# Second gate half and value compression in alternation, the linear attention's output gated and turned in two halves

## The chip, the cores and the metric

The kernel runs on one core of a Trainium2 chip. The metric is the device time of one execution in microseconds (us). The engines that matter are TensorE (PE: products and transposes), VectorE (DVE), ScalarE (ACT) and SyncE (SP), which here only issues loads. Each engine works through its own queue in order and waits on semaphores.

## The reference, cut to what matters

Two transformer layers on 256 tokens with a width of 2048, in float32. The first layer has four branches (pooling, spatial gating, window attention, convolution). The second has a sparse attention with compressed keys and values, a gated linear attention, a cross attention and a feed-forward part. This part of the second layer is what the change touches:

```python
def compress(u, pe, w1, w2):                 # u: 256 tokens, 2 heads; 15 blocks of 32 tokens
    blk = u[:, tok] + pe[None, None, :, None, :]
    blk = blk.transpose(0, 1, 3, 2, 4).reshape(B, n_cmp, HKV, -1)      # 4096 per block and head
    return (jax.nn.silu(blk @ w1) @ w2).transpose(0, 2, 1, 3)
kc = rms_norm(compress(k_cmp, pe_k, w_ck1, w_ck2), g_kc)
vc = compress(v_cmp, pe_v, w_cv1, w_cv2)
...
o_gla = gla_mixer(heads(q_l, GLA_HEADS) * (GLA_DK ** -0.5), heads(k_l, GLA_HEADS),
                  heads(v_l, GLA_HEADS), heads(log_a, GLA_HEADS))
o_gla = rms_norm(o_gla, g_gla_out).astype(x.dtype).reshape(B, T, -1) * jax.nn.silu(r_l)
x = x + jnp.concatenate([o_nsa, o_gla], axis=-1) @ w_out
```

Here `r_l` comes out of the layer's input projection, and is 1024 wide; the kernel makes it in two halves of 512 columns, `rl0` and `rl1`.

## The kernel before, in words

**Weights in chunks.** All large products are a list of `units` (one for each weight block, mostly 512 columns wide), and each unit is cut into `chunks` of 512 KB. One list, `chunks`, sets the order in which SP loads them, ScalarE and VectorE split them, and TensorE multiplies by them. A chunk lands in one of `NR` = 5 raw buffers (`raw`). ScalarE writes a rounded high part (`whi`, L404) and VectorE the rest (`wlo`, L405), into one of `NH` = 4 slots. TensorE then makes three products for each of two operand tiles and two halves of the tokens (L464): 12 for a chunk. The raw buffer is free once VectorE is done (`raw_free`), the slot once TensorE is. A chunk is split when TensorE's place in the list is at most four chunks before it.

**The compression's chunks.** `ck1` and `cv1` (keys and values, 8 chunks each) are used as they come, without a split: TensorE reads the raw buffer itself (`rows=32`, L422, eight instructions a chunk), so the raw buffer is freed by TensorE. Both read one operand buffer, `kp`. VectorE fills it for the keys, and again for the values (L1483) when ck1's last product is done. The result of cv1 is copied by ScalarE into `hid` (`use_hid`, L1150), and TensorE then folds it (`small_out`, L1492), the first step to the compressed values.

**PSUM banks.** Banks 0 to 3 belong to the units: a unit takes banks 2i and 2i + 1 with i the parity of its index, one for each half of the tokens. Its first product in a bank waits until the unit before it of the same parity has been read out (`slot_free`). Banks 4 to 7 are for the background work.

**Order around the change.** The units of the second layer's input projection are ql, ga, kl, vl0, vl1, q0, q1, ksvs, kcvc, kwvw, ck1, rl0, rl1, cv1. The eight chunks of ck1 alternate with the eight of rl0; then come the eight of rl1, and then the eight of cv1. The units wl0 to wl3 follow (`w_out` with the linear attention's half of its rows), then wp0 to wp3 (the sparse attention's half). wl0 has four chunks: its first two need operand tiles 0 to 3, the others tiles 4 to 7.

**Background threads.** Everything else is written as Python generators (`gla`, `compress`, `nsa_part` and others). `step()` advances each of them once, several times in a chunk, and so puts their instructions between the products; it does nothing while the planned clock of VectorE is over 3 us (`AHEAD`) ahead of TensorE's. The planner keeps a clock `now` for each engine, from estimated durations, and each signal has a due time (`when`). A thread holds an instruction back with `ready` until the due time of what it needs is 0.6 us past on TensorE's clock. If a chunk needs what is not yet written, `step(True)` advances all threads until it is. A load has no due time so far: it counts as landed.

**The end of the linear attention.** For each half `i`, once `rl{i}` and two heads' norms are there, `gla` multiplies the head outputs `vl` by the gate (L1443). When both halves are done it turns the result: `turn_seq` transposes two tiles at a time (L332) and splits them into the operand `oop` (ScalarE L314, VectorE L318). `oop` lies where the projection's operand lies, so a tile of it may only be written when rl1's product with the old tile is done (`hop_free`, set for the unit `LAST_IN2`, which is rl1).

**The names in the trace.** `t_raw`, `t_whi`, `t_wlo` are the weight buffers; `t_A` holds the operands; `t_H` here `vl` and `rl`; `t_Y0b` has `kp`; `t_R` has `hid`; `ps` is any PSUM bank.

Of the kernel before, what the change touches and what calls it, by code (L numbers as in the profile page):

```python
# [13 lines left out]
P = 128  # L14
# [38 lines left out]
for _i in range(4):  # L53
    for _n in range(4):
        S1[f"g{_i}{_n}"] = (10496 + _i * D + _n * 512, 10496 + _i * D + _n * 512 + 512)
S2 = dict(ql=(2584, 3096), kl=(3096, 3608), vl0=(3608, 4120), vl1=(4120, 4632), rl0=(4648, 5160), rl1=(5160, 5672),
          q0=(0, 512), q1=(512, 1024), kcvc=(1024, 1536), ksvs=(1536, 2048), kwvw=(2048, 2560))
# [9 lines left out]
def due(tok):  # L67

    if tok is None:
        return 0.0  # L70
    if isinstance(tok, list):
        return max([due(x) for x in tok] + [0.0])
    return tok[0].when.get(tok[1], 0.0)


def elements(pattern):
    n = 1
    for _, size in pattern.ap[1:]:
        n *= size
    return n  # L80
# [23 lines left out]
class Lane:  # L104
# [41 lines left out]
    def dma(self, out, in_, count, *tokens):  # L146
        self.wait(*tokens)
        count.value += 16
        self.engine.dma_start(out, in_).then_inc(count.sem, 16)
        return (count, count.value)  # L150


def build(nc, dr, out):
    ctx = ExitStack()
    with ctx:
        body(nc, dr, out, ctx)


def body(nc, dr, out, ctx):
# [39 lines left out]
    def at(reg, shape, dt=F32, off=0, name=None):  # L199
        names[0] += 1  # L200
        return nc.alloc_sbuf_tensor_at(name or f"t{names[0]}_{reg}", [P] + list(shape), dt, offset=where[reg] + int(off))
# [7 lines left out]
    def par(name, a=0, b=None):  # L209
        lo, hi = PP[name]  # L210
        return pp[:, lo + a:(hi if b is None else lo + b)]
# [14 lines left out]
    def ready(*toks):  # L226

        while max([due(x) for x in toks]) > T.now - 0.6:
            yield
# [12 lines left out]
    flags = {}  # L242
# [61 lines left out]
    def split_into(op, kt, n, src, tok, scale=1.0, scales=None, behind=None):  # L304

        if scales is None:
            a = S.do(lambda e: e.activation(op.hi[:, kt:kt + n, :], src, ACT.Copy, scale=scale), tok, behind)  # L307
            b = V.do(lambda e: e.scalar_tensor_tensor(out=op.lo[:, kt:kt + n, :], in0=src, scalar=scale,  # L308
                                                      in1=op.hi[:, kt:kt + n, :].bitcast(F32), op0=ALU.mult,
                                                      op1=ALU.subtract), a, behind)  # L310
        else:
            for k in range(n):
                sc = scales(kt + k)
                a = S.do(lambda e, k=k, sc=sc: e.activation(op.hi[:, kt + k, :], src[:, k, :], ACT.Copy, scale=sc),  # L314
                         tok, behind)
            for k in range(n):
                sc = scales(kt + k)
                b = V.do(lambda e, k=k, sc=sc: e.scalar_tensor_tensor(  # L318
                    out=op.lo[:, kt + k, :], in0=src[:, k, :], scalar=sc, in1=op.hi[:, kt + k, :].bitcast(F32),
                    op0=ALU.mult, op1=ALU.subtract), a, behind)  # L320
        for k in range(n):
            op.ready[kt + k] = b
        return b

    def turn_start(c, kt, src, tok):

        b = c.bank()
        ps = banks[b][:].rearrange("p (k n) -> p k n", k=2)
        T.wait(tok)
        for k in range(2):  # L330
            for t in range(NT):
                fn = lambda e, k=k, t=t: e.transpose(ps[:, k, t * P:(t + 1) * P], src(t, kt + k), ident)  # L332
                if k == 1 and t == 1:
                    got = T.do(fn)
                else:
                    T.silent(fn)
        return b, ps, got

    def turn_seq(c, op, kts, src, tok, scale=1.0, scales=None, behind=None, over=None):

        def finish():
            k0, b, ps, got = pend.pop()
            held = behind if over is None else [over[k0], over[k0 + 1]]
            c.tok = bg_free[b] = split_into(op, k0, 2, ps, got, scale, scales, held)

        pend = []
        for kt in kts:
            if len(c.pool) == 1 and pend:
                finish()
            while over is not None and kt + 1 not in over:  # L350
                yield
            yield from ready(tok, *[bg_free[b] for b in c.pool if len(c.pool) == 1])
            pend.insert(0, (kt,) + turn_start(c, kt, src, tok))
            if len(pend) > 1:
                finish()
            yield
        finish()


    units, chunks = [], []  # L360

    def unit(name, w, n, kts, op, use, rows=None, need=(), k0=0, flip=False):


        u = dict(name=name, w=w, n=n, kts=kts, op=op, use=use, rows=rows, index=len(units),
                 need=need, k0=k0, flip=flip)
        per = w.shape[2]
        assert kts % per == 0 and per * n <= 1024, (name, kts, per, n)
        for c in range(kts // per):
            chunks.append((u, c, per))  # L370
        units.append(u)
# [18 lines left out]
    hop_free = {}  # L390
# [728 lines left out]
    vl = at("H3", [NT, 1024])  # L1119
    rl = at("H4", [NT, 1024])  # L1120
    nq = at("M0", [NT, 1024])
    kcvc = at("M1", [NT, 512])
    ksvs = at("M1", [NT, 512], off=4096)
    kwvw = at("R0", [NT, 512])

    def rscale(t):
        return keepers[:, 2 + t:3 + t]

    def keep2(dst, name):
        def use(t, ps, tok):  # L1130
            d = dst(t)
            n = d.shape[-1]
            r = S.do(lambda e: e.activation(d, ps[:, 0:n], ACT.Copy, scale=rscale(t)), tok, last_use["rx"],
                     last_use["free2"])
            last_use[name] = r
            return r
        return use

    def in2(name, n, use):
        unit("2" + name, dr["w_in2"][name], n, 16, hop, use, need=("x1",))  # L1140
# [22 lines left out]
    def use_rl(i):  # L1163
        def use(t, ps, tok):
            d = rl[:, t, i * 512:(i + 1) * 512]
            a = S.do(lambda e: e.activation(d, ps[:], ACT.Tanh, scale=half_r[:, t:t + 1]), tok, last_use["rx"],
                     last_use["free2"])
            r = V.do(lambda e: e.scalar_tensor_tensor(out=d, in0=d, scalar=1.0, in1=ps[:], op0=ALU.add,
                                                      op1=ALU.mult), a)
            last_use[f"rl{i}"] = r  # L1170
            return r
        return use

    units2 = dict(
        ql=lambda: in2("ql", 512, keep2(lambda t: qlkl[:, t, 0:512], "ql")),
        kl=lambda: in2("kl", 512, keep2(lambda t: qlkl[:, t, 512:1024], "kl")),
        ga=lambda: unit("2ga", dr["w_in2"]["ga"], 40, 16, hop, use_ga, need=("x1",), flip=True),
        q0=lambda: in2("q0", 512, keep2(lambda t: nq[:, t, 0:512], "nq0")),
        q1=lambda: in2("q1", 512, keep2(lambda t: nq[:, t, 512:1024], "nq1")),
        vl0=lambda: in2("vl0", 512, keep2(lambda t: vl[:, t, 0:512], "vl0")),  # L1180
        vl1=lambda: in2("vl1", 512, keep2(lambda t: vl[:, t, 512:1024], "vl1")),
        kcvc=lambda: in2("kcvc", 512, keep2(lambda t: kcvc[:, t, :], "kcvc")),
        ksvs=lambda: in2("ksvs", 512, keep2(lambda t: ksvs[:, t, :], "ksvs")),
        kwvw=lambda: in2("kwvw", 512, keep2(lambda t: kwvw[:, t, :], "kwvw")),
        rl0=lambda: in2("rl0", 512, use_rl(0)),
        rl1=lambda: in2("rl1", 512, use_rl(1)),
        ck1=lambda: unit("ck1", dr["w_ck1"], 256, 32, lambda l: kp[:, l, :], use_hid("k"), rows=32),
        cv1=lambda: unit("cv1", dr["w_cv1"], 256, 32, lambda l: kp[:, l, :], use_hid("v"), rows=32, need=("hk",)))
    for name in "ql ga kl vl0 vl1 q0 q1 ksvs kcvc kwvw ck1 rl0 rl1 cv1".split():
        units2[name]()  # L1190


    at_ = next(i for i, x in enumerate(chunks) if x[0]["name"] == "ck1")
    chunks[at_:at_ + 16] = [chunks[at_ + 8 * j + i] for i in range(8) for j in range(2)]

    bT = at("Y1b", [4, 256])
# [13 lines left out]
    oop = Operand("A", 16)  # L1210
# [5 lines left out]
    def gla():  # L1216
        c = CG
# [111 lines left out]
        made, summed = {}, {}  # L1329
# [110 lines left out]
        for i in range(2):  # L1440
# [3 lines left out]
                out=vl[:, t, i * 512:(i + 1) * 512], in0=vl[:, t, i * 512:(i + 1) * 512], scalar=rscale(t),  # L1444
                in1=rl[:, t, i * 512:(i + 1) * 512], op0=ALU.mult, op1=ALU.mult) for t in range(NT)],
                after=last_use[f"rl{i}"])
            yield
        if "nsa4" in flags:
            c.pool = [4, 5]
        yield from turn_seq(c, oop, range(0, 8, 2), lambda t, k: vl[:, t, k * P:(k + 1) * P], c.tok,  # L1450
                            scales=lambda k: par("g_gla", k % 2, k % 2 + 1), over=hop_free)

        yield from norm(c, ckv[0][:].rearrange("p t (h d) -> p (t h) d", d=P), qlkl[:, 0, :].rearrange("p (h d) -> p h d", d=P))
        a = c.v(lambda e: e.tensor_scalar(par("g_cq"), par("g_cq"), P ** -0.5, None, ALU.mult))
# [392 lines left out]
    for d in range(len(chunks)):  # L1847
        u, c, per = chunks[d]
# [170 lines left out]
```

## Time and profile before

| | |
|---|---|
| runs | 2429.7, 2432.16, 2433.64 us, median 2432.16 |
| the profiled execution | 2432.07 us, its span 2430.7 us |
| TensorE busy | 2401.1 us (99%), granted clock 0.995 in the mean |
| VectorE, ScalarE busy | 1502.8 us (62%), 1118.3 us (46%) |
| loads | 186 GB/s in the mean |

The span is the time from the first to the last instruction of the execution that was profiled. A busy share of 99% says that what TensorE does in turn sets the time. Times below are us from the span's start. A line of a timeline has the start, the duration, engine, source line, operation, what is written and read, and the count; in brackets stands idle time before it with what ended it. Products overlap one another, so the starts give their pace, not the durations.

### The profile page before, as it was taken

Reading aid. Unit: us, or ns where it says so; the run is one execution under the profiler, and the core shown is the slowest. Engines: PE = TensorE matmul, PEld = TensorE weight load, DVE = VectorE, ACT = ScalarE, POOL = GpSimd, SP = SyncE. Lnnn points to the kernel's source line nnn. Section 1 sums busy time; section 2 is a strip of 40 time slices with the busy share of each in tenths; the row PEclk is TensorE's granted clock in tenths of the full one; section 3 lists DMA queues with packets and bytes.
Section 4 is the critical chain, followed back from the end, with each engine's and each line's share of the span. In section 5 each row is a group of like instructions: output and inputs, shape, how many; then the busy total and the mean of one; then the engine's idle time right before and its main releaser. Section 6 shows DMA issues by size and latency. Waiting matters only on the chain.

```text
span 2430.7 us, 28661 instructions
## 1 busy us (share of the span) xinstructions
PE 2401.1 (99%) x11302; PEld 1985.0 (82%) x11302; DVE 1502.8 (62%) x2122; ACT 1118.3 (46%) x1391; POOL 0.2 (0%) x4
## 2 busy tenths in 40 slices
PE   8999999999999999999999999998999999999999
PEld 7888888888888888888888887787888888888887
DVE  5566989865544554577667865776555555554443
ACT  5554444544444444454455654445444444444333
POOL 0000000000000000000000000000000000000000
PEclk9999999999999999999999999999999999999999
DMA  8545666666665766665544444553666666666664
GB/s 292 173 143 185 192 191 194 213 184 214 191 198 151 257 225 198 191 217 181 176 156 149 163 135 166 163 178 126 189 190 187 190 190 189 190 191 190 200 203 143
DMA packets 124227, 452.99 MB, mean 186 GB/s; under 512 B 13691, under 2 KB 15916, under 8 KB 123068
## 3 DMA queue, kind: packets, MB, share of 16 engines
q1 hardware_dynamic: 124092, 451.17, 60.0%
q8 instruction: 88, 1.44, 0.2%
q14 instruction: 47, 0.39, 0.0%
HBM read 448.99 MB, written 2.12 MB: 186 GB/s over the span
## 4 chain that ended last, share of the span: by engine, by line
PE 97%; DVE 1%; DMA 1%; ACT 1%; issue 0%; SPq 0%; DVEq 0%; ACTq 0%
PE ps L464 90%; PE ps L332 1%; PE ps L599 1%; PE ps L549 1%; PE ps L1408 1%; PE ps L582 0%; DVE t_wlo L405 0%; PE ps L513 0%; DMA t_raw<-w_out 0%; PE ps L989 0%; ACT t_whi L404 0%; PE ps L422 0%; PE ps L445 0%; DMA t_raw<-w_kv 0%; PE ps L1540 0%; PE ps L1578 0%
## 5 line engine op out<-in xcount | busy, mean ns | idle before, releaser
L464 PE MATMUL ps<-t_whi,t_A 128*128 128x512 f32 (+1 forms) x4992 | 1552.8, 393 | 10.2 <-DVE t_wlo L405 9.2
L405 DVE TENSOR_TENSOR t_wlo<-t_raw,t_whi 128x1024 fp32r<-128x1024 f32 x805 | 980.4, 1224 | 807.8 <-ACT t_whi L404 802.5
L404 ACT ACTIVATE t_whi<-t_raw 128x1024 fp32r<-128x1024 f32 x805 | 849.3, 1058 | 1043.5 <-PE ps L464 1026.4
L464 PEld LDWEIGHTS ps<-t_whi,t_A 128*128 128x128 f32 x4992 | 926.7, 189 | 200.9 <-DVE t_wlo L405 9.9
L464 PE MATMUL ps<-t_wlo,t_A 128*128 128x512 f32 (+1 forms) x2496 | 971.7, 389 | 0.0
L464 PEld LDWEIGHTS ps<-t_wlo,t_A 128*128 128x128 f32 x2496 | 470.6, 189 | 97.8
L464 PE MATMUL ps<-t_whi,t_Y0a 128*128 128x512 f32 x1152 | 355.9, 390 | 1.2 <-DVE t_wlo L405 1.2
L464 PEld LDWEIGHTS ps<-t_whi,t_Y0a 128*128 128x128 f32 x1152 | 215.3, 188 | 45.6 <-DVE t_wlo L405 1.7
L464 PE MATMUL ps<-t_wlo,t_Y0a 128*128 128x512 f32 x576 | 224.2, 389 | 0.0
L464 PEld LDWEIGHTS ps<-t_wlo,t_Y0a 128*128 128x128 f32 x576 | 108.1, 188 | 22.6
L883 DVE SCALAR_TENSOR_TENSOR t_Y1a<-t_H,t_pp,t_Y1a 128x255 f32<-128x255 f32 (+29 forms) x240 | 96.3, 465 | 0.0
L464 PE MATMUL ps<-t_whi,t_Y1a 128*128 128x512 f32 x256 | 79.3, 391 | 0.0
L464 PEld LDWEIGHTS ps<-t_whi,t_Y1a 128*128 128x128 f32 x256 | 47.6, 188 | 9.5
L464 PE MATMUL ps<-t_wlo,t_Y1a 128*128 128x512 f32 x128 | 49.8, 389 | 0.0
L332 PEld LDWEIGHTS ps<-t_cc,t_H 128*128 128x128 f32 x184 | 23.3, 145 | 10.6 <-DVE t_Y0a L308 2.5
L332 PE MATMUL ps<-t_cc,t_H 128*128 128x128 f32 x184 | 28.7, 281 | 2.3 <-DVE t_Y0a L308 1.6
L464 PEld LDWEIGHTS ps<-t_wlo,t_Y1a 128*128 128x128 f32 x128 | 24.0, 188 | 5.0
L308 DVE SCALAR_TENSOR_TENSOR t_Y0a<-ps,t_Y0a 128x512 fp32r<-128x512 f32 x30 | 20.5, 687 | 12.0 <-ACT t_Y0a L307 12.0
L307 ACT ACTIVATE t_Y0a<-ps 128x512 fp32r<-128x512 f32 x30 | 17.6, 589 | 19.5 <-PE ps L332 19.5
L698 ACT ACTIVATE t_W<-ps 128x512 f32<-128x512 f32 x32 | 19.1, 598 | 16.0 <-PE ps L464 16.0
L570 ACT ACTIVATE t_H<-t_H,t_st 128x128 f32<-128x128 f32 (+1 forms) x32 | 14.3, 447 | 23.7 <-DVE t_st L563 23.7
L314 ACT ACTIVATE t_A<-ps,t_pp 128x256 fp32r<-128x256 f32 x48 | 19.8, 470 | 9.9 <-PE ps L332 9.9
(290 smaller groups left out, 1097.5 us busy)
## 6 DMA issues: line engine op xcount, KB each, us to landing
t_raw<-w_in SPq DMA_DIRECT2D x376, 512.0 KB, 4.1
t_raw<-w_gu SPq DMA_DIRECT2D x176, 512.0 KB, 3.6
t_raw<-w_down SPq DMA_DIRECT2D x88, 512.0 KB, 4.2
t_raw<-w_branch SPq DMA_DIRECT2D x64, 512.0 KB, 4.1
t_raw<-w_out SPq DMA_DIRECT2D x64, 512.0 KB, 4.1
t_raw<-w_ck SPq DMA_DIRECT2D x16, 512.0 KB, 4.2
t_raw<-w_cv SPq DMA_DIRECT2D x16, 512.0 KB, 4.6
t_raw<-w_cq SPq DMA_DIRECT2D x8, 512.0 KB, 3.9
```

Of the source, the lines that this page charges most:

```text
L307: a = S.do(lambda e: e.activation(op.hi[:, kt:kt + n, :], src, ACT.Copy, scale=scale), tok, behind)
L308: b = V.do(lambda e: e.scalar_tensor_tensor(out=op.lo[:, kt:kt + n, :], in0=src, scalar=scale, in1=op.hi[:, kt:kt + n, :].bitcast(F32), op ...
L314: a = S.do(lambda e, k=k, sc=sc: e.activation(op.hi[:, kt + k, :], src[:, k, :], ACT.Copy, scale=sc), tok, behind)
L332: fn = lambda e, k=k, t=t: e.transpose(ps[:, k, t * P:(t + 1) * P], src(t, kt + k), ident)
L404: a = S.do(lambda e: e.activation(whi[:, s, 0:n], raw[:, d % NR, 0:n], ACT.Copy), tok, free)
L405: b = V.do(lambda e: e.tensor_tensor(wlo[:, s, 0:n], raw[:, d % NR, 0:n], whi[:, s, 0:n].bitcast(F32), ALU.subtract), a, free)
L464: fn = lambda e, x=x, w=w, kt=kt, k=k, t=t, j=j, bk=bk: e.matmul(bk[:, 0:n], x[:, u["k0"] + kt, t * P:(t + 1) * P], w[:, k, :], start=(kt ...
L549: c.pe([lambda e, h=h: e.matmul(banks[b][:, h * nk:(h + 1) * nk], scores(h)[0], scores(h)[1], start=True, stop=True) for h in range(nh)])
L599: c.pe([lambda e, h=h, k=k: e.matmul(banks[b][:, h * w:(h + 1) * w], PT[:, (h * nkt + k) * P:(h * nkt + k + 1) * P], values(h, k), start=( ...
L698: last_use[f"G{t}"] = S.do(lambda e: e.activation(G[:, t, :], ps[:], ACT.Tanh, scale=0.5), tok, last_use.get(f"G{t}"))
L883: fns.append(lambda e, x=x, y=y, w=w: e.scalar_tensor_tensor(out=y, in0=x, scalar=w, in1=y, op0=ALU.mult, op1=ALU.add))
L1408: summed[h, j] = c.pe([lambda e, i=i, w=w: e.matmul(ps3[:, :, i:16], con("sel", 16 - i, 144 - i), w, start=(i == 0), stop=(i == 15), skip_ ...
```

## The change

There are three edits. The units come in the order ck1, rl0, cv1, rl1, and the chunks of cv1 alternate with those of rl1, as those of ck1 do with rl0. In `gla` the turn moves into the loop over halves: half 0 is gated and its four tiles are turned and split, then half 1. In the planner, a load gets a due time: SP's clock, which advances by the load's size at 320 GB/s, plus 2 us. No instruction is added or taken away.

```diff
     def dma(self, out, in_, count, *tokens):
         self.wait(*tokens)
         count.value += 16
-        self.engine.dma_start(out, in_).then_inc(count.sem, 16)
+        made = self.engine.dma_start(out, in_)
+        self.now = max(self.now, due(list(tokens))) + elements(made.ins.outs[0]) * made.ins.outs[0].ap[0][1] / 80000
+        count.when[count.value] = self.now + 2.0
+        made.then_inc(count.sem, 16)
         return (count, count.value)
...
-    for name in "ql ga kl vl0 vl1 q0 q1 ksvs kcvc kwvw ck1 rl0 rl1 cv1".split():
+    for name in "ql ga kl vl0 vl1 q0 q1 ksvs kcvc kwvw ck1 rl0 cv1 rl1".split():
         units2[name]()


     at_ = next(i for i, x in enumerate(chunks) if x[0]["name"] == "ck1")
+    chunks[at_:at_ + 16] = [chunks[at_ + 8 * j + i] for i in range(8) for j in range(2)]
+
+    at_ = next(i for i, x in enumerate(chunks) if x[0]["name"] == "cv1")
     chunks[at_:at_ + 16] = [chunks[at_ + 8 * j + i] for i in range(8) for j in range(2)]
...
                 in1=rl[:, t, i * 512:(i + 1) * 512], op0=ALU.mult, op1=ALU.mult) for t in range(NT)],
                 after=last_use[f"rl{i}"])
             yield
-        if "nsa4" in flags:
-            c.pool = [4, 5]
-        yield from turn_seq(c, oop, range(0, 8, 2), lambda t, k: vl[:, t, k * P:(k + 1) * P], c.tok,
-                            scales=lambda k: par("g_gla", k % 2, k % 2 + 1), over=hop_free)
+            if "nsa4" in flags:
+                c.pool = [4, 5]
+            yield from turn_seq(c, oop, (4 * i, 4 * i + 2), lambda t, k: vl[:, t, k * P:(k + 1) * P], c.tok,
+                                scales=lambda k: par("g_gla", k % 2, k % 2 + 1), over=hop_free)
```

## Rows read from the trace of the kernel before

**Rows 1.** The page: the span, and each engine's busy time.

```profile
span 2430.7 us, 28661 instructions
...
PE 2401.1 (99%) x11302; PEld 1985.0 (82%) x11302; DVE 1502.8 (62%) x2122; ACT 1118.3 (46%) x1391; POOL 0.2 (0%) x4
```

**Rows 2.** TensorE's waits in all: engine, line, releaser; total us, times, longest.

```profile
PE ps L1492 <- ACT t_R L1150: 4.2, 1, 4.2
...
PE ps L422 <- DMA t_raw<-w_cv: 2.6, 2, 2.0
```

**Rows 3.** Stretches: length, busy time of PE, PEld, DVE, ACT, POOL; clock; DMA; GB/s.

```profile
1434.00:1477.00 43.00, 43.00 (x262) 32.21 (x261) 30.53 (x69) 24.59 (x54) 0.00 (x0) 1.00 0.68 233
...
1501.90:1508.70 6.80, 6.80 (x30) 6.51 (x30) 3.15 (x10) 1.09 (x2) 0.00 (x0) 0.50 0.00 0
...
1509.90:1525.50 15.60, 8.05 (x79) 3.93 (x77) 6.76 (x10) 6.05 (x10) 0.00 (x0) 0.79 0.86 318
...
1515.50:1518.90 3.40, 3.25 (x21) 1.30 (x22) 0.00 (x0) 0.04 (x1) 0.00 (x0) 0.50 1.00 406
...
1525.50:1529.50 4.00, 4.00 (x15) 3.21 (x15) 2.54 (x6) 1.42 (x5) 0.00 (x0) 0.54 0.89 312
```

**Rows 4.** Timeline of TensorE from rl1's end to wl0.

```profile
1509.74 0.40 PE L464 MATMUL ps<-t_wlo,t_A 128*128 128x512 f32 x1
1510.07 2.37 PE L422 MATMUL ps<-t_raw,t_Y0b 128*32 128x256 f32 x40
1514.39 0.64 PE L422 MATMUL ps<-t_raw,t_Y0b 128*32 128x256 f32 x8 [1.96 <-DMA t_raw<-w_cv]
...
1523.63 1.06 PE L1492 MATMUL ps<-t_cc,t_R 128*128 128x30 f32 x4 [4.17 <-ACT t_R L1150]
1525.49 1.19 PE L464 MATMUL ps<-t_whi,t_A 128*128 128x512 f32 x2 [0.81 <-DVE t_A L318]
...
1529.04 0.67 PE L332 MATMUL ps<-t_cc,t_H 128*128 128x128 f32 x4
1529.46 0.71 PE L464 MATMUL ps<-t_whi,t_A 128*128 128x512 f32 x2
```

**Rows 5.** Timeline of SP: the loads issued when cv1's products free buffers.

```profile
1510.77 1.28 SPq L149 DMA_DIRECT2D t_raw<-w_cv  x3
```

**Rows 6.** Timeline of ScalarE at rl0's end and after rl1's.

```profile
1475.64 1.25 ACT L1166 ACTIVATE t_H<-ps,t_st 128x512 f32<-128x512 f32 x2
...
1518.86 1.06 ACT L404 ACTIVATE t_whi<-t_raw 128x1024 fp32r<-128x1024 f32 x1 [7.99 <-DMA t_raw<-w_out]
...
1523.21 0.37 ACT L1150 ACTIVATE t_R<-ps 128x256 f32<-128x256 f32 x1
...
1528.00 0.84 ACT L314 ACTIVATE t_A<-ps,t_pp 128x256 fp32r<-128x256 f32 x2 [1.91 <-PE ps L332]
```

**Rows 7.** Timeline of TensorE: a ck1 chunk, and rl1's first chunk (1472.12 to 1474.86).

```profile
1437.84 0.39 PE L464 MATMUL ps<-t_wlo,t_A 128*128 128x512 f32 x1
1438.16 0.64 PE L422 MATMUL ps<-t_raw,t_Y0b 128*32 128x256 f32 x8
1438.73 0.73 PE L464 MATMUL ps<-t_whi,t_A 128*128 128x512 f32 x2
...
1472.12 0.62 PE L464 MATMUL ps<-t_whi,t_A 128*128 128x512 f32 x2
...
1474.86 0.62 PE L464 MATMUL ps<-t_whi,t_A 128*128 128x512 f32 x2
```

**Rows 8.** Timeline of VectorE at rl0's end and after rl1's.

```profile
1468.28 2.02 DVE L1483 TENSOR_TENSOR t_Y0b<-t_M,t_pp 128x240 f32<-128x240 f32 x4
...
1476.34 1.28 DVE L1168 SCALAR_TENSOR_TENSOR t_H<-t_H,ps 128x512 f32<-128x512 f32 x2 [1.74 <-ACT t_H L1166]
...
1511.62 1.42 DVE L1443 SCALAR_TENSOR_TENSOR t_H<-t_H,t_st,t_H 128x512 f32<-128x512 f32 x2
...
1528.87 0.88 DVE L318 SCALAR_TENSOR_TENSOR t_A<-ps,t_pp,t_A 128x256 fp32r<-128x256 f32 x2 [1.46 <-ACT t_A L314]
```

## The prediction

> **What bounds the kernel now.** The page's busy line comes first: TensorE is busy for 2401.1 of 2430.7 us [rows 1], so all its idle time is 29.6 us and only what shortens TensorE's own queue, or ends a wait in it, can count. The waits of TensorE come next. Two of them stand in one place: 4.2 us in front of the fold of the value compression (L1492) and 2.6 us in front of its chunks [rows 2]. The table by stretches shows that place: from 1509.9 to 1525.5 us TensorE is busy for 8.05 of 15.60 us, and the 4.0 us after it run at a granted clock of 0.54 [rows 3].
>
> TensorE's timeline shows why [rows 4]. The last chunk of the second gate half (rl1) begins its last matmul at 1509.74. Five chunks of cv1, which stood ready in the five raw buffers, pass in 2.37 us. A raw buffer of such a chunk is freed by TensorE itself, so the sixth load is issued only at 1510.77 [rows 5], and its matmuls begin at 1514.39. Behind it come the loads of w_out: its first split starts on ScalarE at 1518.86 after 7.99 us of idling [rows 6], and the first product of wl0 at 1525.49. In short, eight chunks that need no split drain both stages (raw and whi/wlo), and these are filled again from nothing.
>
> **What the alternation takes away.** The first two chunks of wl0 will have been loaded and split while rl1 and cv1 still run. From the end of rl1's last product (1509.74 plus 0.23, a twelfth of the 2.74 us from 1472.12 to 1474.86 [rows 7], the pace of a chunk's twelve products) to 1525.49 are 15.5 us. The work in them stays, at these prices. In the ck1/rl0 stretch a chunk of this kind starts at 1438.16, the next group at 1438.73, and the group before it began 0.32 before it, where 0.23 is usual: 0.57 + 0.09 = 0.66 us [rows 7], eight times 5.3 us. (In a row five took 2.37 us, 0.47 each; the 1.5 us more is the price of alternating.) Two turns of four transposes at 0.42 (1529.04 to 1529.46) [rows 4] are 0.8, the fold 0.4. That makes 6.5, so 9.0 us go. The slow clock behind the waits goes too: 4.00 us at 0.54 [rows 3] are 1.8 us. Together 10.8 us. The half clock from 1501.9 to 1508.7 has no wait in it (TensorE is busy for all 6.80 us [rows 3]); what stands there stays, and I count nothing for it.
>
> **What it adds.** Four costs, all waits in TensorE's queue.
>
> *The banks of rl1.* A unit takes its pair of banks from the parity of its index. So far the order ck1, rl0, rl1, cv1 gives rl1 the banks of ck1, which were long free. Now the order ck1, rl0, cv1, rl1 gives rl1 the banks of rl0, with one cv1 chunk (0.66) between. Its first product waits until VectorE has finished rl0's tanh product of that bank. In this trace rl0 ends at 1472.12 [rows 7]; the tanh runs at 1475.64 [rows 6] and the product of the first half ends at about 1476.98 (half of the 1.28 from 1476.34) [rows 8]. At 1472.78 rl1 would have waited 4.2 us for it; with no queue on ScalarE and VectorE, nothing. Those are the bounds. Both queues were behind there partly since, at that seam, two more chunks come within the four of lookahead at once; with alternating chunks only two of the next four need a split. That takes up to 2.4 us (two of VectorE's 1.2) off the lag: 1.8. I take 2.0. Behind the waiting product stand all of TensorE's instructions, those of the two attentions among them, and SP's next loads, which wait for the raw buffers that the cv1 chunks free.
> The Trainium skill (Perfetto Trace Analysis, under Optimizing Tensor Performance, Matmuls) advises that independent groups should rotate through PSUM banks, so that emptying one overlaps the next group's products. The trace agrees as far as the 4.2 us go, and by the rule alone the sum would have 4.2 in place of 2.0.
>
> *The clock.* In the rows of before, a wait of 1.96 us is soon followed by 3.40 us at 0.50 [rows 3, 4]. So the bank wait costs between nothing and 1.7 us more. I take 0.8, the middle.
>
> *The fold (L1492).* It is put into TensorE's queue at once when cv1 ends, and waits for ScalarE's copy of the hidden row, 0.37 us [rows 6]. With the two signals that is 0.5 at least; 1.6 if a split (1.06) is ahead in ScalarE's queue; the 4.2 of now comes since ScalarE waits there for w_out. I take 0.9.
>
> *The second half's turn.* wl0's third chunk needs columns that can only be gated once rl1 has ended. Now: end of rl1 1510.14; gate done 1511.62 + 1.42 = 1513.04 [rows 8], 2.9 later; a turn's transposes 0.4; its split on ScalarE and VectorE 1528.00 to 1528.87 + 0.88 = 1.8 [rows 6, 8]. With some 0.3 for signals, 5.4 us. Cover: two chunks of wl0 at 2.74 (1472.12 to 1474.86) [rows 7] and the turns, 6.2 us. So nothing at best; with a weight split ahead on both engines (1.06 + 1.22) 1.5 more than the cover, and with the planner's 0.6 us of caution and other late threads 3. I take 1.2. The first half's turn moves into rl1's time, where its four operand tiles come free after rl1's second chunk: eight transposes that were always there, and their splits, beside 37 us of products. Nothing, and 0.8 us if it had to stand at the end.
>
> The two further moves that cost nothing: kp for the values is written by VectorE from 1468.28 for 2.02 us [rows 8], done at 1470.3, before rl0's last product (1472.12), so cv1 finds it ready; without that cover it is 2 us. And the number of loads is the same, 16 chunks through the same queue; no load is put before another engine's work.
>
> *The planner.* Loads now have a due time, so waits on them push its clocks of ScalarE, VectorE and TensorE, everywhere in the kernel. A raw buffer is reloaded five chunks (13.7 us) ahead, and the due time adds 1.6 + 2.0 us, so in steady stretches it binds nothing; at seams a thread's step moves by a chunk. I take 0 and bound it by 2.5 us each way, as all idle time outside this place is 22.0 us (29.6 less 7.6) [rows 1, 3].
>
> **Sum.** -10.8 + 2.0 + 0.8 + 0.9 + 1.2 = -5.9 us. The profiled execution took 2432.07 us (span 2430.7), the median of the runs is 2432.16, so that is 2426.2 us, 0.24% less. A change of 0.2%, 4.9 us, is about what can be told from none.
>
> **Rivals.**
> *The bank wait is paid in full* (the page's rule above): 4.2 with its 1.7 of slow clock give -10.8 + 4.2 + 1.7 + 0.9 + 1.2 = -2.8, 2429.3 us, no change that can be told. For it: rl0's end shows just that lag. Against it: fewer splits are ahead there, and attention work of TensorE falling between covers part. 0.20.
>
> *The turn of the second half is late*: the thread is stepped only when wl0 asks, other threads are forced along, and wl0 waits as long as the fold does now, 4.2 in place of 1.2, with 1.7 of clock: -1.2, 2430.9 us. Against it: the gate follows rl1 by 2.9 us already. 0.08.
>
> *The alternation starves* (slower): a rl1 chunk's buffer comes free with the cv1 chunk five before it. Load 3.6 (issue 1510.77, used 1514.39), split 1.06 + 1.22 and 0.4 of signals make 6.3 us, against two pairs, 2 x (2.74 + 0.66) = 6.8. If a split of another chunk stands ahead on both engines (2.3), each of seven chunks waits 1.8: +12.6, and -5.9 becomes +6.7, 2438.8 us. It decides from 1.6 us a chunk. Against it: ck1/rl0 alternates in the same way, and TensorE is busy there 43.00 of 43.00 us at 233 GB/s [rows 3]. 0.05.
>
> *The planner's due times shift threads for the worse elsewhere* by 5 us or more: about 2431 us, or above 2437 from 11 us on. 0.09, of which 0.04 slower.
>
> *The forecast's case* has 0.58; its own range is 2421 to 2428.5, and it is nearly all beyond 0.2%.
>
> **Chances and range.** Faster 0.58 with 0.01 from a lucky planner; slower 0.05 + 0.04 = 0.09; the rest, 0.32, the same. Range: down to all costs at their least (-10.8 + 0.5, 2421.8) and 1.3 of planner's luck, 2420.5; up to the late turn with the planner against it, 2433.0.
>
> **What would show it.** Right: no wait of TensorE on w_cv; wl0's first product right behind rl1's last; the L1492 wait under 2 us; TensorE's idle time about 7 us less in sum with a full clock from there to 1540. A wait of L464 on the tanh product (L1168) just after the first cv1 chunk sizes the first cost; one on L318 at wl0's third chunk the fourth. Wrong: waits of L464 on the split (L405) between rl1's chunks, or new idle time far from here.

## The result, and the profile after

The changed kernel takes 2427.23 us (median of 17 runs, 2424.5 to 2429.08) beside 2432.31 us for the kernel before (17 runs): a ratio of 0.9979, interval 0.9971 to 0.9986, or 5.1 us less. In a later group, beside the experiments, the ratio was 0.9974 (0.9963 to 0.9985). The forecast was 5.9 us less. The experiments will show that the size came right while the forecast gave it to the wrong edit.

In the profiled execution (2428.58 us) the page begins like this, to be laid beside [rows 1]:

```profile
span 2427.3 us, 28656 instructions
...
PE 2400.5 (99%) x11302; PEld 1982.4 (82%) x11302; DVE 1502.9 (62%) x2122; ACT 1118.8 (46%) x1391; POOL 0.2 (0%) x4
```

TensorE's idle time, the span less its busy time, fell from 29.6 to 26.8 us. A further part of the gain is the clock: the stretches at a granted clock of 0.50 add up to 25.8 us in the profiled execution of before and to 19.0 us in this one. These are TensorE's waits, most of which stand far from the change (beside [rows 2]). The load's due time added three lines to the file and the new order three more, so L464 is L467 now, L1168 is L1171 and L1492 is L1498:

```profile
PE ps L467 <- DVE t_wlo L408: 10.7, 4, 8.1
PE ps L552 <- DVE t_st L493: 3.2, 1, 3.2
PE ps L467 <- DVE t_H L1171: 2.9, 1, 2.9
...
PE ps L1498 <- ACT t_R L1153: 1.6, 1, 1.6
```

The wait on w_cv has gone, and so has the one on the turned operand (L318, 0.8 us). The fold's wait for the copy of the hidden row has shrunk from 4.2 to 1.6 us, and one of 2.9 us for rl0's tanh product has come; both were foreseen. TensorE's timeline has them in place (beside [rows 4, 7]):

```profile
1474.01 0.40 PE L467 MATMUL ps<-t_wlo,t_A 128*128 128x512 f32 x1
1474.34 0.64 PE L425 MATMUL ps<-t_raw,t_Y0b 128*32 128x256 f32 x8
1477.84 1.20 PE L467 MATMUL ps<-t_whi,t_A 128*128 128x512 f32 x2 [2.87 <-DVE t_H L1171]
...
1518.25 0.64 PE L425 MATMUL ps<-t_raw,t_Y0b 128*32 128x256 f32 x8
1520.47 0.63 PE L1498 MATMUL ps<-t_cc,t_R 128*128 128x30 f32 x4 [1.59 <-ACT t_R L1153]
1520.94 0.71 PE L467 MATMUL ps<-t_whi,t_A 128*128 128x512 f32 x2
...
1525.08 0.91 PE L467 MATMUL ps<-t_whi,t_A 128*128 128x512 f32 x2
```

rl0's last product starts at 1474.01, one cv1 chunk follows, and then rl1 waits for the bank. At the other end the last cv1 chunk, the fold and the last rl1 chunk (1520.94 to 1525.08) follow one another. wl0's first product stands at 1525.08, right behind rl1, where 15.5 us lay before. What rl1 waits for are rl0's tanh on ScalarE (L1169) and its product on VectorE (L1171); VectorE's line above that product is the write of kp for the values, which is done at 1472.21, before cv1 begins (beside [rows 6, 8]):

```profile
1476.40 1.24 ACT L1169 ACTIVATE t_H<-ps,t_st 128x512 f32<-128x512 f32 x2
```

```profile
1470.21 2.00 DVE L1489 TENSOR_TENSOR t_Y0b<-t_M,t_pp 128x240 f32<-128x240 f32 x4
...
1477.10 1.28 DVE L1171 SCALAR_TENSOR_TENSOR t_H<-t_H,ps 128x512 f32<-128x512 f32 x2 [1.73 <-ACT t_H L1169]
```

ScalarE is free of the attention's exponentials (L573) only at 1476.40, and VectorE's first half is done at 1477.74. The stretches, with the granted clock in the third column from the right (beside [rows 3]):

```profile
1211.70:1215.10 3.40, 3.40 (x10) 2.63 (x9) 2.22 (x3) 1.79 (x2) 0.00 (x0) 0.50 0.31 123
...
1477.90:1481.30 3.40, 3.40 (x12) 3.01 (x13) 3.16 (x6) 1.49 (x4) 0.00 (x0) 0.50 0.41 167
1505.20:1508.60 3.40, 3.40 (x16) 1.75 (x16) 1.55 (x4) 1.35 (x2) 0.00 (x0) 0.50 0.00 0
1508.60:1522.30 13.70, 12.11 (x70) 8.29 (x69) 7.12 (x10) 5.42 (x6) 0.00 (x0) 1.00 0.87 283
1522.30:1525.70 3.40, 3.40 (x10) 2.62 (x9) 1.95 (x3) 1.33 (x4) 0.00 (x0) 0.50 1.01 387
1525.70:1560.00 34.30, 34.30 (x185) 27.21 (x184) 28.10 (x38) 17.80 (x27) 0.00 (x0) 1.00 0.46 139
```

Each wait has 3.4 us at half clock behind it, by estimate a loss of 1.7 us more; for the fold's wait that is so in this execution and not in a second one (last section). From 1525.7 on TensorE is never idle and at full clock up to 1560, where before it was slow for 4 us behind wl0's start, and once more for 3.4 us from 1549.7. The first row, at 1211.7, is far from any edit; the last section comes back to it.

### The profile page after: what moved, and what is told of

Same layout as the page of the kernel before. It is cut to its first block, busy times and chain, and to the rows that moved or that the text cites. A ratio compares the mean times of both kernels' runs of the same rounds, so it can differ in the third digit from the quotient of the medians.

```text
span 2427.3 us, 28656 instructions
## 1 busy us (share of the span) xinstructions
PE 2400.5 (99%) x11302; PEld 1982.4 (82%) x11302; DVE 1502.9 (62%) x2122; ACT 1118.8 (46%) x1391; POOL 0.2 (0%) x4
## 4 chain that ended last, share of the span: by engine, by line
PE 97%; DVE 2%; ACT 1%; DMA 0%; issue 0%; SPq 0%; DVEq 0%; ACTq 0%
PE ps L467 89%; PE ps L335 1%; PE ps L602 1%; PE ps L552 1%; PE ps L1414 1%; DVE t_wlo L408 1%; PE ps L585 0%; PE ps L516 0%; ACT t_whi L407 0%; PE ps L992 0%; PE ps L425 0%; PE ps L448 0%; DMA t_raw<-w_kv 0%; PE ps L1584 0%; DVE t_st L489 0%; DMA t_raw<-w_in 0%
## 5 line engine op out<-in xcount | busy, mean ns | idle before, releaser
L467 PE MATMUL ps<-t_whi,t_A 128*128 128x512 f32 (+1 forms) x4992 | 1554.0, 393 | 12.5 <-DVE t_wlo L408 9.4
L407 ACT ACTIVATE t_whi<-t_raw 128x1024 fp32r<-128x1024 f32 x805 | 849.5, 1058 | 1037.5 <-PE ps L467 1020.5
L467 PEld LDWEIGHTS ps<-t_whi,t_A 128*128 128x128 f32 x4992 | 927.2, 189 | 205.0 <-DVE t_wlo L408 10.3
L467 PE MATMUL ps<-t_wlo,t_A 128*128 128x512 f32 (+1 forms) x2496 | 972.1, 389 | 0.0
L467 PEld LDWEIGHTS ps<-t_wlo,t_A 128*128 128x128 f32 x2496 | 470.8, 189 | 98.3
L467 PE MATMUL ps<-t_whi,t_Y0a 128*128 128x512 f32 x1152 | 355.8, 390 | 1.2 <-DVE t_wlo L408 1.2
L467 PEld LDWEIGHTS ps<-t_whi,t_Y0a 128*128 128x128 f32 x1152 | 215.3, 188 | 45.7 <-DVE t_wlo L408 1.7
L467 PE MATMUL ps<-t_wlo,t_Y0a 128*128 128x512 f32 x576 | 224.2, 389 | 0.0
L467 PEld LDWEIGHTS ps<-t_wlo,t_Y0a 128*128 128x128 f32 x576 | 108.1, 188 | 22.5
L467 PE MATMUL ps<-t_whi,t_Y1a 128*128 128x512 f32 x256 | 79.4, 391 | 0.0
L467 PEld LDWEIGHTS ps<-t_whi,t_Y1a 128*128 128x128 f32 x256 | 47.6, 188 | 9.5
L467 PE MATMUL ps<-t_wlo,t_Y1a 128*128 128x512 f32 x128 | 49.8, 389 | 0.0
L467 PEld LDWEIGHTS ps<-t_wlo,t_Y1a 128*128 128x128 f32 x128 | 24.0, 188 | 5.0
L573 ACT ACTIVATE t_H<-t_H,t_st 128x128 f32<-128x128 f32 (+1 forms) x32 | 14.3, 447 | 23.8 <-DVE t_st L566 23.7
```

Source lines behind the costliest of these rows:

```text
L407: a = S.do(lambda e: e.activation(whi[:, s, 0:n], raw[:, d % NR, 0:n], ACT.Copy), tok, free)
L467: fn = lambda e, x=x, w=w, kt=kt, k=k, t=t, j=j, bk=bk: e.matmul(bk[:, 0:n], x[:, u["k0"] + kt, t * P:(t + 1) * P], w[:, k, :], start=(kt ...
```

## The experiments

Each group of four ran on one chip beside the kernel before, and a ratio is to before on that chip. The first group has no due times, due times only, rl0 quiet and fold held; the second the changed kernel again, turn in one piece, rl1 first, and quiet and fold; the third the other four. The recorded ratio is near the quotient of the means, so it differs a little from that of the medians. Its interval is about 0.001 to each side, 2.4 us, so kernels whose ratios lie closer than that are not told apart, least of all across groups. The last column is the time, in the profiled execution, from ck1's first product to the first wait of the cross attention (L513), less the same for the kernel before (1434.64 to 1654.21, 219.57 us). That takes the seam by itself, but in one execution only.

| kernel | order | halves | due times | median us | ratio (interval) | seam us |
|---|---|---|---|---|---|---|
| changed, first measured | x | x | x | 2427.23 | 0.9979 (0.9971 to 0.9986) | -4.9 |
| changed, second group | x | x | x | 2426.03 | 0.9974 (0.9963 to 0.9985) | -6.4 |
| no due times | x | x | | 2430.96 | 0.9991 (0.9982 to 1.0000) | -2.8 |
| due times only | | | x | 2431.30 | 0.9996 (0.9987 to 1.0005) | -2.0 |
| turn in one piece | x | | x | 2431.81 | 1.0000 (0.9990 to 1.0010) | +3.2 |
| halves only | | x | | 2426.95 | 0.9975 (0.9965 to 0.9984) | -4.4 |
| order only | x | | | 2434.56 | 1.0008 (0.9999 to 1.0016) | +1.9 |
| due times from ck1 on | x | x | part | 2428.30 | 0.9981 (0.9973 to 0.9990) | -6.6 |
| rl0 quiet | x | x | x | 2424.37 | 0.9961 (0.9949 to 0.9974) | -9.7 |
| fold held | x | x | x | 2425.69 | 0.9975 (0.9964 to 0.9986) | -6.7 |
| rl1 first | x | x | x | 2422.99 | 0.9960 (0.9948 to 0.9972) | -8.9 |
| quiet and fold | x | x | x | 2428.24 | 0.9980 (0.9971 to 0.9990) | -7.8 |
| rl1 first and fold | x | x | x | 2427.09 | 0.9976 (0.9967 to 0.9986) | -7.2 |

The kernel before had medians of 2434.19, 2433.78 and 2433.66 us in the three groups.

**No due times.** The changed kernel with the load's due time taken out:

```diff
-        made = self.engine.dma_start(out, in_)
-        self.now = max(self.now, due(list(tokens))) + elements(made.ins.outs[0]) * made.ins.outs[0].ap[0][1] / 80000
-        count.when[count.value] = self.now + 2.0
-        made.then_inc(count.sem, 16)
+        self.engine.dma_start(out, in_).then_inc(count.sem, 16)
```

> The changed kernel with loads that have no due time again (order of units and chunks, and the turn in halves, stay). If the gain comes from the alternation alone, this is within 1.5 us of the changed kernel, 2426 to 2429 us, with the wait on L1168 in front of rl1 (2 to 4 us) and the one in front of the fold (about 1.6 us) still there. If the planner's due times made part of it, it is 2 us or more slower than the changed kernel.

The ratio is 0.9991, so 3 to 4 us of the gain (0.9979 and 0.9974) went with the due times. The timeline shows a wait that the changed kernel does not have:

```profile
1474.65 0.64 PE L422 MATMUL ps<-t_raw,t_Y0b 128*32 128x256 f32 x8 [1.87 <-DVE t_Y0b L1486]
1478.65 1.22 PE L464 MATMUL ps<-t_whi,t_A 128*128 128x512 f32 x2 [3.36 <-DVE t_H L1168]
```

```profile
1471.51 1.23 DVE L405 TENSOR_TENSOR t_wlo<-t_raw,t_whi 128x1024 fp32r<-128x1024 f32 x1 [2.11 <-ACT t_whi L404]
1472.66 1.94 DVE L1486 TENSOR_TENSOR t_Y0b<-t_M,t_pp 128x240 f32<-128x240 f32 x4
```

```profile
1469.44 0.51 ACT L570 ACTIVATE t_Y1a<-t_Y1a,t_st 128x256 f32<-128x256 f32 x1 [5.88 <-DVE t_st L569]
...
1470.44 1.05 ACT L404 ACTIVATE t_whi<-t_raw 128x1024 fp32r<-128x1024 f32 x1
```

VectorE's write of kp stands behind a weight split that waits 2.11 us for ScalarE's half of it (L404). That half does not wait for its load, which had landed by 1466.4. It stands in ScalarE's queue behind the attention's exponentials (L570), which start at 1469.44 when VectorE's t_st is there. In the changed kernel the split (L407) runs at 1466.96, ahead of the exponentials, and the write of kp is not held up. So here cv1's first chunk waits 1.87 us, and rl1 3.36 us in place of 2.87. The due times change this order on both engines; what decides it inside the planner was not looked at step by step.

**Due times only**, the same edit made to the kernel before.

> The kernel before with due times for loads and nothing else. By the forecast's step (worth 0, bound 2.5 us either way) it is within 0.1% of before, with the drained stretch before wl0 as it was: about 7.6 us of idle time of TensorE in it. If the due times are the gain, it is 3 us or more faster than before.

0.9996, within 0.1% as forecast, and the drained stretch is there. The due times are worth nothing by themselves.

**rl0 quiet.** The changed kernel, without background steps inside rl0's last chunk:

```diff
         if forced:
             T.now += 0.3
+        elif "quiet" in flags:
+            return
...
+        if u["name"] == "2rl0" and (c + 1) * per == u["kts"]:
+            flags["quiet"] = True
         pe_chunk(d)
+        flags.pop("quiet", None)
```

> The changed kernel, but no background step is made during rl0's last chunk, so ScalarE and VectorE have less in front of rl0's tanh and its product. If the wait in front of rl1 (2.87 us, then 3.4 us at half clock) is their queue's and not the banks' alone, it falls under 1 us and the half clock behind it goes: 2 to 4 us faster than the changed kernel, 2423.5 to 2425.5. If the wait is the fixed length of tanh and product behind one short chunk, it stays over 2 us and the time is the changed kernel's.

0.9961 beside 0.9979 and 0.9974, and the median is 2424.37 us (5 runs), as fast as expected. The wait is shorter by 1.1 us, and the clock stays up:

```profile
1473.79 0.73 PE L467 MATMUL ps<-t_whi,t_A 128*128 128x512 f32 x2 [1.76 <-DVE t_H L1171]
```

```profile
1470.00:1480.00 10.00, 8.24 (x51) 5.73 (x50) 6.84 (x15) 4.17 (x11) 0.00 (x0) 1.00 0.61 195
```

It fell to 1.76 us and not under 1 us, so both are at work: the queues of ScalarE and VectorE, and the length of tanh and product behind one short chunk.

**Fold held.** The changed kernel with one more token:

```diff
         i = "kv".index(which)
-        yield from ready(c.tok, c.freed())
+        yield from ready(c.tok, c.freed(), last_use["hid" + which])
```

> The changed kernel, but the fold (L1498 there) is held back until ScalarE's copy of the hidden row is due. The wait of 1.59 us in front of it goes, and if the 3.4 us at half clock that begin 1.9 us later are its consequence, those too: 1.6 to 3.3 us faster, 2424 to 2425.6. If the half clock there has another cause, only 1.6 us or less, 2425.6 to 2427.

0.9975, the changed kernel's own ratio, so the gain of 1.6 us or more did not come. The fold's wait is gone; a new one stands at wl0's third chunk:

```profile
PE ps L467 <- DVE t_A L321: 1.0, 1, 1.0
```

The fold's 1.6 us had covered the second half's turn. TensorE's idle time is 26.6 us where it was 26.8.

**The changed kernel again**, for a comparison on the second chip.

> The changed kernel as it is, on the chip of the other kernels of this group, to compare them with. Ratio to before 0.9979 as measured, a median 4 to 6 us below that of before.

0.9974, as expected.

**Turn in one piece.** The changed kernel with the old form of the turn:

```diff
-            if "nsa4" in flags:
-                c.pool = [4, 5]
-            yield from turn_seq(c, oop, (4 * i, 4 * i + 2), ...
+        if "nsa4" in flags:
+            c.pool = [4, 5]
+        yield from turn_seq(c, oop, range(0, 8, 2), ...
```

> The changed kernel with the turn in one piece again, after both halves are gated. With alternation rl1 ends right before wl0, so all eight transposes' splits are late: wl0's first chunk waits for gate (2.9 us after rl1's end) and first turn (2 us), with only the fold beside it: 3 to 5 us of waiting on L321 in front of wl0 and 1.7 us of half clock, so 4 to 6 us slower than the changed kernel, about as slow as before. If the halves are only a detail, within 1.5 us of the changed kernel.

2431.81 beside 2426.03 us on the same chip, and a ratio of 1.0000: without the halves the gain is gone. The 5.8 us are what was expected. In front of wl0 stand now:

```profile
1525.96 1.09 PE L335 MATMUL ps<-t_cc,t_H 128*128 128x128 f32 x8 [1.97 <-DVE t_H L1449]
1528.46 0.74 PE L467 MATMUL ps<-t_whi,t_A 128*128 128x512 f32 x2 [1.40 <-DVE t_A L321]
```

That is a wait for the gate and one for the first split, 3.4 us of the 5.8; no trace of a typical run shows the rest. The profiled execution was the slowest of twelve (2439.34 us; the median is 2431.81). It has the full clock for 10.9 us behind these waits and then 13.7 us at half clock from 1539.4, so its seam in the table is on the high side.

**rl1 first.** Other banks for the same alternation:

```diff
-... ck1 rl0 cv1 rl1
+... ck1 rl0 rl1 cv1
...
+    at_ = next(i for i, x in enumerate(chunks) if x[0]["name"] == "2rl1")
+    mixed = [chunks[at_ + 8 * j + i] for i in range(8) for j in range(2)]
+    mixed[14], mixed[15] = mixed[15], mixed[14]
+    chunks[at_:at_ + 16] = mixed
+    skew[0] = 1
```

`skew[0]` is added to the index of every later unit.

> The changed kernel with other banks: the units come as ck1, rl0, rl1, cv1 again, so rl1 has the banks of ck1, its chunks alternate with cv1's beginning with rl1 (the last two swapped, so that rl1 still ends last), and all later units take the other pair. Now cv1's first chunk waits for rl0's tanh product, with 2.7 us of rl1 between in place of 0.66. If the banks make the wait in front of rl1, no wait on L1171 over 1 us is left there, and the half clock behind it goes: 2.5 to 4.5 us faster than the changed kernel. If it is another queue that is late there, the wait stays at its place under another name and the time is the changed kernel's within 1 us.

2422.99 us (5 runs) beside 2426.03 us on the same chip, 3.0 us less, at the low end of what was expected. rl1 begins without a wait, and cv1's first chunk has a short one:

```profile
1476.59 0.39 PE L467 MATMUL ps<-t_wlo,t_A 128*128 128x512 f32 x1
1476.82 0.52 PE L1501 MATMUL ps<-t_cc,t_R 128*128 128x30 f32 x4
1477.18 0.64 PE L585 MATMUL ps<-t_cc,t_Y1a 128*128 128x128 f32 x4
1479.11 0.64 PE L425 MATMUL ps<-t_raw,t_Y0b 128*32 128x256 f32 x8 [1.29 <-DVE t_H L1171]
```

The same two instructions of ScalarE and VectorE (L1169, L1171) end it. What has changed is what lies between rl0 and their reader: 0.66 us before, now 2.7 us of rl1 and 1.0 us of background work (L1501, L585). The 1.29 us are left all the same because cv1's first chunk waits for both halves of the product where rl1's waits for the first, 0.64 us less. So the wait in front of rl1 is one for its banks. The second half's turn waits 1.73 us at wl0's third chunk here.

**Quiet and fold** together.

> Both edits of the first group together on the changed kernel: no background step in rl0's last chunk, and the fold held back until its operand is due. If the two waits are separate, the gains add: 4.7 us (quiet) and 1.6 us or a little more (fold) below the changed kernel, 2420 to 2422.5 on a chip where before takes 2432 to 2434. If one wait only moves into the other, no better than quiet alone.

The gains do not add: 2428.24 us, slower than quiet alone (0.9980 beside 0.9961, in another group), and the expectation fell. Without the fold's wait, wl0's third chunk waits 1.3 us for the turn. TensorE's idle time is 25.7 us, less than the 26.7 of rl0 quiet. What makes it slower than its idle time says is the clock. Its profiled execution has six stretches at half clock, 22.8 us in all, rl0 quiet's has two, 7.9 us; half of the difference is 7.5 us, and TensorE's busy time is 7.3 us longer (2401.6 and 2394.3). Three of the six are in the next rows, the last two in the cross attention, where nothing was edited:

```profile
1476.00:1481.00 5.00, 4.73 (x18) 4.02 (x19) 4.69 (x10) 1.02 (x2) 0.00 (x0) 0.66 0.55 202
1651.70:1658.50 6.80, 6.08 (x14) 4.90 (x15) 2.63 (x7) 3.90 (x10) 0.00 (x0) 0.50 0.21 70
1668.70:1672.10 3.40, 3.40 (x9) 2.65 (x9) 0.28 (x1) 0.00 (x0) 0.00 (x0) 0.50 0.00 0
```

**Due times from ck1 on.** The changed kernel, with due times from eight chunks before ck1 to the end of the kernel:

```diff
-        count.when[count.value] = self.now + 2.0
+        if DUE[0]:
+            count.when[count.value] = self.now + 2.0
...
+        DUE[0] = d >= next(i for i, x in enumerate(chunks) if x[0]["name"] == "ck1") - 8
```

> The changed kernel with due times for loads only from eight chunks before ck1's first on; before that a load counts as landed, as in the kernel before. If the 2 to 3 us that the due times are worth beside the alternation come from the seam itself (VectorE's write of kp put ahead of a split that waits for its load), there is no wait on that write in front of cv1's first chunk, and the ratio to before is the changed kernel's, 0.997 to 0.998. If they come from elsewhere in the kernel, it is the ratio without due times, 0.999.

0.9981, at the edge of the expected ratio, and no wait on kp's write. The seam is 6.6 us shorter than before's, like the changed kernel's (4.9 and 6.4) and not like that without due times (2.8). So the due times are not needed ahead of ck1, and what they give shows at this seam. That the split waits for its load, as expected here, is not what the trace without due times shows: ScalarE's order holds it up.

**Halves only**, the turn in halves made to the kernel before.

> The kernel before with the turn in halves and nothing else. Eight cv1 chunks still stand between rl1 and wl0, so the second half's turn is hidden and the drained stretch stays: within 0.1% of before, two turns fewer beside the waits for w_out. A gain of 2 us or more would say that the halves work without the alternation.

This expectation fell, and it is the one that matters most: 0.9975. One edit of three gives as much as all three, as far as the intervals can tell. The cv1 chunks still drain the buffers (the profiled execution took 2430.48 us, the slowest of nine; it has a wait of 1.84 us on a split at 1071.91, far from the edit, with 3.4 us at half clock behind it, which before's does not have):

```profile
1513.26 0.43 PE L464 MATMUL ps<-t_wlo,t_A 128*128 128x512 f32 x1
1513.62 2.37 PE L422 MATMUL ps<-t_raw,t_Y0b 128*32 128x256 f32 x40
1518.09 0.64 PE L422 MATMUL ps<-t_raw,t_Y0b 128*32 128x256 f32 x8 [2.10 <-DMA t_raw<-w_cv]
...
1521.17 0.64 PE L422 MATMUL ps<-t_raw,t_Y0b 128*32 128x256 f32 x8 [0.60 <-DMA t_raw<-w_cv]
1524.77 1.22 PE L464 MATMUL ps<-t_whi,t_A 128*128 128x512 f32 x2 [2.96 <-DVE t_wlo L405]
...
1528.77 0.89 PE L1492 MATMUL ps<-t_cc,t_R 128*128 128x30 f32 x4
```

From rl1's last product (1513.26 + 0.23) to wl0's first are 11.3 us, where [rows 4] have 15.5. wl0's first chunk now waits only for its own weights (L405). Before, the splits of its operand tiles 0 to 3 stood behind those of w_out on ScalarE, and the last of them ended at 1525.35 on VectorE, 0.14 us before wl0's first product:

```profile
1524.48 0.87 DVE L318 SCALAR_TENSOR_TENSOR t_A<-ps,t_pp,t_A 128x256 fp32r<-128x256 f32 x2
```

So the late splits held wl0, and the fold's 4.17 us [rows 4] passed beside them: with the fold alone out of the way wl0 would have begun hardly earlier. By the code the fold stood there since all threads are forced along while wl0 asks for its tiles; with the first half turned during rl1 nothing is forced, and the fold comes at 1528.77 without a wait. No run tests this forcing by itself. From ck1 to the cross attention this execution is 4.4 us shorter than before's: 1.9 us are idle time of TensorE (6.5 and 8.3 us), the rest is busy time, with 13.6 us at half clock in place of 20.4. The waits that the forecast wanted to remove are still there, 2.10, 0.60 and 2.96 us.

**Order only**, the new order of units and chunks made to the kernel before.

> The kernel before with the new order of units and chunks alone: no turn in halves, no due times. With the turn in one piece the gain was gone (ratio 1.000), without due times 2 to 3 us of it. If both add, this is slower than before by 1 to 4 us, with waits of TensorE on kp's write, on rl0's tanh product, on the fold and on the first turn. If they overlap, it is before's time within 1 us.

1.0008 (0.9999 to 1.0016): not faster, and the four waits are all there, 1.9 us for kp, 3.4 for rl1's banks, 1.5 for the fold and 2.0 + 1.0 for the gate and the turn, 9.8 us in all. They take what the full buffers gave (7.6 us of waits in the drained stretch before).

**rl1 first and fold** together.

> The kernel with rl1 first and the banks exchanged (0.9960 of before), with the fold held back as well. Its fold waits 0.3 us only, so holding it back can give 0.3 us and its place; the wait at wl0's third chunk (1.73 us) stays or grows by what the fold covered. Expected: the same as rl1 first within 1 us, 0.996 of before. If the fold's early place costs more than its wait shows, 2 us faster.

Missed: 0.9976, with runs from 2422.3 to 2431.82 us. Gate and turn of the second half hold wl0 up for 0.90 and 2.09 us in place of 1.73, and 6.8 us at half clock begin there. In both cases where the fold was held back and the bank wait was treated as well, the result was slower than without the fold's edit (0.9980 beside 0.9961, 0.9976 beside 0.9960), each time across groups and with intervals that just overlap.

## Why the prediction was right or wrong, point by point

**The sum** (-5.9 us) met -5.1 us; the seam of the two profiled executions of the changed kernel gives -4.9 and -6.4. That it came so near is in part luck. Taken as parts of the whole change, the terms were off by +0.9 (banks), +0.9 and +1.7 (clock at the banks and behind the fold), -1.7 (clock after 1501.9), +0.7 (fold) and -1.2 us (second turn), which add up to 1.3; and the edit that it took for nothing carries the gain.

**The drained buffers.** Right: no wait of TensorE on w_cv or on w_out's split remains, wl0 follows rl1 at once, and the 4 us of slow clock behind its start are gone. TensorE's idle time was to fall by about 7 us in sum and fell by 2.8; the forecast's own waits (2.0 + 0.9 + 1.2 of the 7.6 us come back) leave 3.5, so that sign was written down wrongly and not the sum. But the 10.8 us were booked for the alternation alone, with costs of 4.9. The runs show that the alternation does not collect them: alone its net is nothing (1.0008), with due times nothing (1.0000), with the halves and no due times it is slower than the halves by themselves (0.9991 and 0.9975), and with all three it is level with them (0.9979 and 0.9974).

**The turn in halves** is the step that failed: "Nothing, and 0.8 us if it had to stand at the end." It is worth 5.8 us in the changed kernel, about 6 in the kernel before, and 4 beside the new order without due times (1.0008 and 0.9991). The forecast priced the transposes and splits as TensorE's own work, and did not ask what wl0's first chunk would wait for without them: gate, turn and split one after the other (1.97 + 1.40 us with alternation), or splits that stand behind those of w_out (until 1525.35 in the kernel before). How the 5.8 and 6 us divide into these waits and the clock is not shown.

**The banks of rl1.** The mechanism was right, shown by the kernel with rl1 first. 2.0 us was too little for it: 2.9 us, between the bounds of 0 and 4.2. The relief was 1.3 us and not 2.2: VectorE has one split (1.23 us) fewer in front of the attention's chain and not two, and what stands on ScalarE right in front of the tanh are the exponentials of that chain, not splits; the kernel with rl0 quiet took 1.1 us away. The rule of the Trainium skill on rotating banks (Perfetto Trace Analysis, Optimizing Tensor Performance, Matmuls) would have put 4.2 into the sum. The 2.9 us lie nearer to 2.0, but the rule names what helps: with rl1 in other banks than rl0 the wait in front of rl1 was gone and the kernel 3.0 us faster.

**The clock.** 0.8 us for the bank wait was half of what it was: 3.4 us at 0.50 in both profiled executions, so 1.7, the upper bound. A second such stretch behind the fold (1.7 us, in one of the two) was not in the sum, and a slow stretch after 1501.9, counted at nothing, went from 6.8 to 3.4 us.

**The fold** took 1.6 us where 0.9 stood: the case that was named, with one split of w_out (1.06 us) ahead of the copy on ScalarE.

**The second half's turn** cost nothing where 1.2 us stood. The fold's wait covers it: with the fold held back it is 1.0 us. The two terms should not have been added.

**The planner.** Booked with 0, bounds of 2.5. Alone it is 0 (0.9996). With the alternation it decides whether VectorE's write of kp stands behind a late split. The forecast read from the trace of before that "cv1 finds it ready", with 2 us if not, and did not see that this hangs on the due times: without them it is 1.87 us and its clock. No due times against the changed kernel is 0.9991 against 0.9974 to 0.9979, 3 to 4 us, more than the bound.

**The rivals.** The alternation did not starve: no wait on a split stands between rl1's chunks. The bank wait was paid at 2.9 and not 4.2 us, and the late turn of the second half did not come. That one of the other edits, the halves, does all of it by itself was not among them. The halves with due times and without the alternation were not run, so whether the alternation is worth keeping as written stays open; with rl1 first, or rl0 quiet, the whole is 3.4 to 3.7 us better than the halves alone by the ratios (0.9960 and 0.9961 beside 0.9975), though from different groups of five runs and with intervals that overlap.

## What to carry to other kernels

When a change has several edits on one stretch, ask of each what the next consumer waits for without it, and run each by itself: here the late operand alone was worth the whole gain, and full buffers alone were worth nothing since they brought as many waits as they took. An order that keeps the buffers full also brings producer and consumer closer: look at what bank, copy or scratch buffer the next unit needs, and count the cover between them in microseconds. A wait that covers another is not added to it, and taking it away may give nothing.

## What the runs showed of the hardware that was not expected

The same program has half-clock stretches in different places from one execution to the next. The changed kernel's first profiled execution has the row at 1211.7 shown above, with no wait near it; its second, with the same instructions, has the full clock there. At the cross attention's 3.2 us wait the first has 3.4 us at half clock from 1655.4, behind the wait, and the second 6.8 us from 1649.9, beginning inside it. These rows are of the second:

```profile
1211.70:1215.10 3.40, 3.40 (x16) 2.79 (x16) 1.44 (x2) 2.60 (x3) 0.00 (x0) 1.00 0.18 67
...
1518.50:1522.00 3.50, 3.50 (x18) 2.93 (x18) 2.43 (x4) 2.18 (x4) 0.00 (x0) 1.00 1.00 386
...
1649.90:1656.70 6.80, 5.57 (x13) 4.54 (x14) 2.60 (x8) 3.55 (x9) 0.00 (x0) 0.50 0.24 80
```

The fold waited 1.58 us there too, and no slow stretch followed it. One such stretch is 1.7 us, and the runs of one kernel spread over 4.6 us (2424.5 to 2429.08). So a wait such as the fold's 1.6 us may cost itself, or 1.7 us more, and a single profiled execution does not say which. The bank wait tells the same: at 2.87 and 2.86 us it has such a stretch with it in the two executions of the changed kernel, at 2.89 us it has none in fold held; at 1.76 us it has one in quiet and fold and none in rl0 quiet. Why the kernels with the fold held back and the bank wait treated take longer in more of their runs is not settled.
